# A hybrid decoder step: token rows placed ahead of two weight blocks in SP's queue, and another release for GpSimd's gathers

## The reference

```python
def _rmsnorm(x, g):
    x32 = x.astype(jnp.float32)
    y = x32 * lax.rsqrt(jnp.mean(x32 * x32, axis=-1, keepdims=True) + RMS_EPS)
    return (y * g.astype(jnp.float32)).astype(x.dtype)
...
def _project_in(x, pos, norm_pre, w_in, q_norm, w_q_up, kv_norm, w_kv_up):
    xn = _rmsnorm(x, norm_pre)
    (qa, kvc, kvs, kvw, gn, ga, qd, kvd, krp, gb, ma, mb) = jnp.split(xn @ w_in, IN_OFFSETS, axis=-1)
...
def _compress(kv, pe_cmp):
    blocks = kv.reshape(b, s_pad // CMP_BLOCK, CMP_BLOCK, NSA_KV_HEADS, 2, NSA_HEAD_DIM)
    c = jnp.mean(blocks + pe_cmp[None, None], axis=2)
    return c[..., 0, :], c[..., 1, :]
...
    cmp_past = cache_nsa_cmp[l, page_table].reshape(b, past, NSA_KV_HEADS, 2, NSA_HEAD_DIM)
    kc, vc = _compress(jnp.concatenate([cmp_past, kvc], axis=1), pe_cmp)
```

## Time and profile before

| | us |
|---|---|
| median of 3 runs | 670.59 |
| lowest and highest run | 667.03, 671.28 |
| the profiled execution | 666.29 |
| its span | 664.5 |
| TensorE busy | 650.8 |
| VectorE busy | 446.0 |
| ScalarE busy | 214.4 |
| GpSimd busy | 77.6 |

### The profile page before, as it was taken

The page is one execution under the profiler, slowest core; times in us unless marked ns, Lnnn a source line. Parts: engine busy times, 40 slices in busy tenths (PEclk is TensorE's granted clock), DMA queues, the critical chain, the costliest instruction groups (busy, mean ns, idle before and its releaser), DMA issues.

```text
span 664.5 us, 15351 instructions
## 1 busy us (share of the span) xinstructions
PE 650.8 (98%) x5771; PEld 433.3 (65%) x5771; DVE 446.0 (67%) x1234; ACT 214.4 (32%) x586; POOL 77.6 (12%) x89
## 2 busy tenths in 40 slices
PE   8999999999999998999999999999999999999996
PEld 3444444463466775778777676688788888886443
DVE  2198799676677778866575664637585757648866
ACT  0311321686445455544453542421011111010221
POOL 0344334126000000220201000000000000000010
PEclk9999999999999999999999999999999999999998
DMA  8999999999989999978759789975411112018011
GB/s 332 417 425 422 423 427 403 353 379 273 366 277 381 400 399 412 408 276 326 279 177 373 276 318 359 406 270 222 159 64 64 64 49 78 1 70 343 3 64 63
DMA packets 67587, 179.44 MB, mean 270 GB/s; under 512 B 7513, under 2 KB 16498, under 8 KB 60218
## 3 DMA queue, kind: packets, MB, share of 16 engines
q1 hardware_dynamic: 56088, 125.14, 51.2%
q0 software_dynamic: 8640, 48.90, 18.2%
q10 hardware_dynamic: 2786, 4.42, 1.8%
HBM read 169.38 MB, written 12.72 MB: 274 GB/s over the span
## 4 chain that ended last, share of the span: by engine, by line
PE 88%; DVE 5%; DMA 3%; ACT 2%; issue 1%; SPq 1%; DVEq 0%; ACTq 0%
PE bank L1561 20%; PE bank L978 12%; PE bank L1398 9%; PE bank L1612 7%; PE bank L1259 5%; PE bank L1382 4%; PE bank L1285 4%; PE bank L1269 4%; PE bank L1367 4%; DMA projP<-x 3%; PE bank L1590 2%; PE bank L1142 2%; PE bank L1332 2%; PE bank L1342 1%; PE bank L1220 1%
## 5 line engine op out<-in xcount | busy, mean ns | idle before, releaser
L978 PE MATMUL bank<-W,XG 128*128 128x494 f32 x192 | 83.6, 580 | 0.7 <-DVE projP L1998 0.7
L1871 ACT ACTIVATE projP<-bank,projP 128x128 f32<-128x128 f32 (+3 forms) x96 | 49.8, 525 | 38.5 <-DVE projP L2354 37.8
L2657 DVE TENSOR_TENSOR projP<-projP,bank 128x260 f32<-128x260 f32 x81 | 32.6, 422 | 42.4 <-PE bank L1561 41.6
L1398 PE MATMUL bank<-W 128*128 128x260 f32 x256 | 60.3, 389 | 0.0
L1661 ACT ACTIVATE projP<-bank 128x128 f32<-128x128 f32 (+5 forms) x87 | 33.4, 392 | 82.2 <-PE bank L1561 47.7
L978 PEld LDWEIGHTS bank<-W,XG 128*128 128x128 f32 x192 | 35.2, 192 | 36.5 <-issue 35.0
L1398 PEld LDWEIGHTS bank<-W 128*128 128x128 f32 x256 | 47.3, 190 | 10.6 <-issue 3.5
L1661 ACT ACTIVATE W<-bank 128x512 f32<-128x512 f32 (+2 forms) x69 | 40.2, 582 | 38.3 <-PE bank L1021 13.3
L2354 DVE CUSTOM_DVE_ANT_0 bank<-bank,maskb 128x128 f32<-128x128 f32 (+3 forms) x96 | 45.6, 509 | 8.0 <-PE bank L1259 7.1
L1259 PE MATMUL bank<-W 64*128 64x128 f32 (+7 forms) x192 | 46.0, 466 | 0.7 <-ACT projP L1871 0.7
L821 POOL DMA_INDIRECT ring<-cmp,idxi x32 | 38.6, 1208 | 67.8 <-DVE VV L2065 48.1
(11 more groups left out here) (479 smaller groups left out, 1163.6 us busy)
## 6 DMA issues: line engine op xcount, KB each, us to landing
ring<-latent SPq DMA_DIRECT2D x168, 256.0 KB, 4.9
XG<-latent SPq DMA_DIRECT2D x56, 256.0 KB, 4.4
W<-w_gate SPq DMA_DIRECT2D x12, 1024.0 KB, 5.8
W<-w_attn SPq DMA_DIRECT2D x16, 494.0 KB, 12.2
W<-latent SPq DMA_DIRECT2D x20, 256.0 KB, 5.3
rope_rows<-ring SPq DMA_DIRECT2D x16, 256.0 KB, 4.4
ring<-win SPq DMA_DIRECT2D x8, 512.0 KB, 7.7
ring<-w_out SPq DMA_DIRECT2D x2, 2048.0 KB, 11.8
```

The costliest lines, as they stand in the source:

```text
L978: mm = pe.matmul(bank[2 * (u % 2) + n][:, 0:GW], XG[:, k * TOK + tl * P:k * TOK + (tl + 1) * P], w_part(half, k, n), start=(k == 0), stop= ...
L1398: mm = pe.matmul(bank[6][:, 0:HALF], gate_w[g % 2][:, at:at + P], X2[:, k * TOK + hf * HALF:k * TOK + (hf + 1) * HALF], start=(k == 0), st ...
L1871: act.activation(Pb[u % 4][:, 0:w], bank[u % 2][:, 0:w], ACT.Exp, bias=NMp[:, u:u + 1], scale=-1.0, accum_out=RSp[:, u:u + 1]).then_inc(S[ ...
L2657: dve.tensor_tensor(out, a, pair_bank(v, product)[:, 0:HALF], ALU.add).then_inc(S["z_by_dve"], 1)
```

## The change

In SP's program the two loads of token rows now stand ahead of the weight blocks 6 and 7. In GpSimd's program the first gather waits for `xtok_in` of 32 where it waited for `w_in7`. No instruction is added or removed.

```diff
                     sp.dma_start(XG[:, k * TOK:k2 * TOK], t["xT"][:, k * TOK:k2 * TOK]).then_inc(S[f"xT_in{r}"], 16)
+                if k == 6:
+                    sp.dma_start(xtok.rearrange("p (t c) -> p t c", t=TILES), t["x"][0:SEQ].rearrange("(t p) c -> p t c", p=P)).then_inc(S["xtok_in"], 16)
+                    sp.dma_start(xdec[0:DEC], t["x"][SEQ:TOK]).then_inc(S["xtok_in"], 16)
                 sp.dma_start(W[:, k * 2 * GW:(k + 1) * 2 * GW], t["w_attn"][:, k, 0:2 * GW]).then_inc(S[f"w_in{k}"], 16)
-            sp.dma_start(xtok.rearrange("p (t c) -> p t c", t=TILES), t["x"][0:SEQ].rearrange("(t p) c -> p t c", p=P)).then_inc(S["xtok_in"], 16)
-            sp.dma_start(xdec[0:DEC], t["x"][SEQ:TOK]).then_inc(S["xtok_in"], 16)
...
             pool.wait_ge(S["idx"], 1)

-            pool.wait_ge(S["w_in7"], 16)
+            pool.wait_ge(S["xtok_in"], 32)
```

## The result

| | before | after |
|---|---|---|
| median, us | 667.68 (666.24 to 674.68, 20 executions) | 671.80 (668.91 to 677.36, 20 executions) |
| profiled execution, us | 666.29 | 676.62 |
| its span, us | 664.5 | 674.8 |

The ratio is 1.0064, 95% interval 1.0045 to 1.0084: about 4.3 us longer (0.64% of 667.68; the interval is 3.0 to 5.6 us), where 1.0 us was forecast. 671.8 lies 0.2 us from the time that I named, but only because the runs I started from had a median of 670.59 and the runs of before beside the result had 667.68. What has to be explained is the difference. The profiled execution is one of the longer of the 20, 10.3 us over that of before, so it shows the mechanism at its largest. In the lines of after, what lies behind the edit has a number one higher (L978 is now L979).

A forecast was written before the change was run, and what follows sets the result against it. TensorE was taken to bound the kernel (98% busy): 0.7 us won at the third tile, B of 1.7 us less 0.5 and 0.2 us of slack gave +1.0 us, 670.59 to 671.6 us; range 666.5 to 676.5.

The forecast's parts named there:

- The token rows move up: SP's queue: token rows land at 22.7 instead of 25.65, closing PE's gap before the third tile: -0.7 us.
- Blocks 6 and 7 move back: SP's queue: the blocks land near 23.6 and 24.8, with slack 3.1 and 5.2 us before PE wants them; nothing lost.
- GpSimd's wait, B: First gather starts at 23.6, 2.7 us later; DMA engines idle for B = 1.7 us (0.7 to 2.8).
- that term (2.0): First gather on GpSimd: 2.0 us from its start to its first bytes, putting these at 25.6.
- What B costs at PE's averages: Sums B late from 77.65 on; the fifth average has 1.5 us slack, so PE loses 0.2 and keeps -0.5.
- Stall 0.2 us: PE's wait at the fifth average, from a sum 1.7 us late against 1.5 us of slack.
- The slack at w_k: ACT's copy at 138.56: w_k landed at 137.7 to 138.1, leaving 0.5 us slack (0.4 to 0.9).
- Behind 143 us nearly all of the chain is PE's own work, so I let the sum stand: After w_k: PE's delay of +1.0 us at 143 us carries unchanged to the end of the kernel.
- rival 1: First gather: no idle time in the DMA, B is 0, PE keeps -0.7 us: 669.9 us; chance 0.25.
- rival 2: First gather: bytes follow issue by 1.0 us on empty engines, B = 0.7, sum 0.0: 670.6 us; chance 0.15.
- rival 3: SP's queue: 32 KB issue delays blocks 6 and 7, leaving a hole up to 3.9 us: +3.2, 673.8 us; chance 0.05.
- Rival 4: w_k: whole delay reaches PE, B 2.8, no slack, L1138 2.6 us late: 673.2 us; chance 0.10.

The follow-up runs named there:

- the split: The changed kernel with the token rows' load cut in two of 256 rows, the first gather released by the first half: 666.08 us beside 666.48, ratio 1.0006.
- The repeated run: The changed kernel itself timed once more, nothing altered: 672.60 us, ratio 1.0103 (1.0076 to 1.0130) against the kernel before.
- the run that kept PE busy: The changed kernel with eight unused matmuls on constants put in front of L1111, where PE waits: 670.85 us, ratio 1.0086.
- the weights ahead: The changed kernel with w_qup and w_k issued between the first two rope stores instead of behind both: 667.71 us beside 666.48, ratio 1.0007.
- the old order with block 5: The kernel before, in its own order of loads, with gathers released by weight block 5 instead of block 7: 670.90 us, ratio 1.0062.
- the split with the weights ahead: The changed kernel with token rows cut in two, gathers released by the first half, and w_qup and w_k ahead of the second rope store: 666.79 us, ratio 1.0010.
- the release by block 5: The changed kernel with the first gather released by weight block 5 instead of the token rows: 665.40 and 665.82 us, ratios 0.9989 and 0.9990.
- the control: The kernel before with w_qup and w_k issued between the two rope stores: 666.30 us, ratio 1.0008 (0.9990 to 1.0026).

## Why the prediction was right in its mechanism and too low in its size

*The token rows move up: right.* The squares began at 23.37 and tile 0's eviction at 31.81, released by PE, and PE's gap closed. The step had the rows land at 22.7: 0.6 us early.

*Blocks 6 and 7 move back: right.* No wait of PE for them. (Their issues left SP at 9.24 and not near 12.) Their cover is larger than the step used: even with the gathers ahead of them PE did not wait.

*GpSimd's wait, B: too low.* 1.7 us (0.7 to 2.8) was forecast; the engines moved 1.36 MB less, 3.2 us, outside even those bounds. Of the terms, the gather started at 24.14 and not 23.6. Its first bytes came between 25.5 and 26.0, 1.4 to 1.9 us after its start: that term (2.0) was good, even a little high. What the step lacked is that bytes don't arrive at full rate once they arrive: 0.04 and 0.16 MB in the next two half microseconds where 0.21 would be full, and that SP's queue thinned out before it ended (0.11 and 0.03 MB in 24 to 25 us, and 376 GB/s in 20 to 24 where before has 415). I had computed a hole with sharp edges. The Trainium skill ("DMA: Bandwidth & Descriptors", section "Latency and other measured facts") gives about 1 us to the first byte on GpSimd's path; after's row, on engines that had nearly run dry, has 1.4 to 1.9 us, so the skill's figure was too short here by 0.4 to 0.9 us, and by it the forecast would have been further off.

*What B costs at PE's averages: too low.* "Stall 0.2 us" came from one average with a known slack. Two were late, by 1.29 and 0.71 us, 2.0 in all, and PE was at +1.3 and not at -0.5. The first of them lies at 57 us, where I had assumed that sums are late only from 77.65 on. In after the sums wait for gathers from 43.48 on, 10.6 us in all.

*The slack at w_k: too high.* 0.5 us was worked out from a byte count; the split's row shows some 0.2. Its smallness is why the 0.7 us that the change wins could not be kept in any kernel. In the profiled execution w_k was later still than B explains: w_qup left 3.7 us later than before (130.35, 126.66), ACT waited until 144.86, some 6.5 us after w_k's landing in before. The repeated run had 142.18, 3.9 us later, about what the late issue explains. The rest, 2.7 us, goes for the most part with the sharing of the engines from 132 to 134 us; why that differs stays open.

*"Behind 143 us nearly all of the chain is PE's own work, so I let the sum stand": the step that failed.* The amount of work stands, the speed does not. Behind PE's wait the granted clock fell to 0.50 and 3.9 us more were lost. That the idle time brings this fall is shown by the run that kept PE busy: nearly the same wait for w_k, clock 1.00, span 3.7 us shorter. It is not the only thing that brings one: twice the clock fell at PE's short matmuls with no wait (the weights ahead; the old order with block 5). The Trainium skill ("TensorE: Matmul & The Clock Gate", section "HAM oscillation — how this bites in real kernels") tells of just this, a stream of matmuls that waits for a transfer and goes on at half the clock, and the traces agree (0.50 behind 5.17 us); I had not weighed it. The 20 executions of after fit it: the nine with a mean clock of 0.996 or more have a median of 669.93 us, 2.2 us over before's 667.68 and near the upper end (2.1) of the forecast; the eleven below have 674.60. The comparison is uneven, for 667.68 is over all executions of before, and before has low clocks, too (673.28 us at 0.990 in a later batch). That the lower clocks of after arise at this same place in each execution is argued from the profiled ones, not shown.

*The rivals.* No hole (rival 1) and the short delay (rival 2) fall with the dent. Late blocks (rival 3) did not occur. Rival 4, the whole delay at PE with B 2.8 and no slack at w_k, was the nearest to what happened; it had 0.10 and should have had the larger chance, and its +2.6 us still lacked the clock.

## What to carry to other kernels

Release a transfer by the point at which its first bytes are needed on the queue, some microseconds before the queue ahead of it runs dry, and not by the landing of the last load ahead of it (in the new order the two releases that lost nothing came some 3 and 6 us before that). Where a stretch follows that the DMA engines saturate, an idle microsecond of theirs is one that every later transfer inherits, even if nobody waits at the time. Look first at what still stands in the queue ahead: in the old order, with the token rows there, the early release cost 5 us. Follow such a delay to the load with the least slack, however far on (here 120 us), and cost PE's idle time there with the clock that it may lose behind it. And a gain of a few tenths at one place is worth nothing while the next transfer has less slack than that: three kernels here (the split, the split with the weights ahead, the release by block 5) removed the 0.7 us gap and kept the bytes, and none was measurably faster.

## What the runs showed of the hardware that I had not expected

- The granted clock of TensorE went from 1.00 to 0.50 (1.2 GHz) behind idle times of PE of 2.17, 2.66, 2.86, 3.95, 4.03 and 5.17 us in five profiled executions, and in after was back at 1.00 some 9 us after PE had resumed (147.18 to about 156). Behind the gap of 0.70 us in before, and of 1.29 and 0.71 us in after, it did not fall; nor did it behind one of 2.56 us at 401 us in the control (1.00 in every stretch from 398 to 410 us). So the length of the gap alone does not decide.
- It can fall with no gap at all: to 0.50 in 137 to 140 us with the weights ahead and in 142 to 145 us in the old order with block 5, while PE was busy throughout with short matmuls. Both lost 1.5 us there. In the other eleven profiled executions the same matmuls ran at 1.00. No run here tells what decides it.
- How long the first gather's bytes take from its start depends on what stands ahead of them: 4.1 to 4.9 us in the three executions with release by block 5 (start at 18.3 to 18.6), 2.6 to 3.1 us in before, and 1.4 to 1.9 us in after, on engines about to run dry. There they need another microsecond to reach the full rate.
- The same load, issued 0.3 us apart in two executions of one kernel, let ACT start 2.7 us apart (144.86 and 142.18), in a stretch in which the DMA engines are busy in both. GpSimd's queue had 0.29 MB of 132 to 134 us in the one and nothing in the other.
